# Two load slots for the later modulation's chunks on TensorE, its additions spread anew, and the rotary angles ahead of x

## The reference

```python
for l in range(DEPTH):                                  # DEPTH = 2
    mod = c_act @ w_ada[l] + b_ada[l]                   # c_act = silu(c), one row of 2048; w_ada 2048 x 6144
    shift, scale, gate = jnp.split(mod, 3, axis=-1)
    h = _layernorm(x) * (1.0 + scale[:, None, :]) + shift[:, None, :]
    p = h @ w_in[l]
    u_f, z_f, cq, ckv, k_r, z_a = jnp.split(p, split_pts, axis=-1)
    y_f = _fourier_mix(u_f, w_fmix[l]) * jax.nn.silu(z_f)
    ...                                                 # 8 heads of latent attention, rotary angles from positions
    y = jnp.concatenate([y_f, y_a], axis=-1) @ w_out[l]
    x = _layernorm(DEEPNORM_ALPHA * x + gate[:, None, :] * y, ln_g[l], ln_b[l])
```

## Time and profile before

| | |
|---|---|
| median of 3 runs | 2257.72 us (2253.89 to 2260.4) |
| the profiled execution | 2257.66 us, its span 2255.9 us |
| mean granted clock of TensorE | 0.956 |
| TensorE busy | 2078.6 us (92%) |
| VectorE, ScalarE busy | 1391.3 us (62%), 921.5 us (41%) |
| transfers | 462.27 MB, mean 205 GB/s |

### The profile page before, as it was taken

One profiled execution on the slowest core, in us unless ns is written; L12 is line 12 of the kernel. 1 busy time (PEld: TensorE's weight loads), 2 busy tenths in 40 slices (PEclk: granted clock), 3 DMA queues, 4 the chain that ended last, 5 costly groups with the idle time before them and its releaser, 6 DMA issues.

```text
span 2255.9 us, 37129 instructions
## 1 busy us (share of the span) xinstructions
PE 2078.6 (92%) x14348; PEld 1879.9 (83%) x14348; DVE 1391.3 (62%) x1913; ACT 921.5 (41%) x1355; POOL 26.2 (1%) x53
## 2 busy tenths in 40 slices
PE   6997986887799999879999899999999999999998
PEld 2786875755799997779998899879989989988986
DVE  5365564656657886678899655555545545545555
ACT  2353343412354454344334333445434434434443
POOL 0000000000000000000000000000000000000000
PEclk8998998988899999989999999999999999999999
DMA  9966665676356764525454455553555555555553
GB/s 392 397 262 230 232 249 205 233 280 250 136 201 231 259 230 180 185 96 185 171 184 150 153 182 185 187 205 132 187 202 184 183 193 186 186 192 192 183 196 130
DMA packets 64205, 462.27 MB, mean 205 GB/s; under 512 B 7120, under 2 KB 7632, under 8 KB 8176
## 3 DMA queue, kind: packets, MB, share of 16 engines
q1 hardware_dynamic: 57152, 410.49, 49.5%
q0 software_dynamic: 6960, 50.46, 6.1%
HBM read 458.83 MB, written 2.10 MB: 204 GB/s over the span
## 4 chain that ended last, share of the span: by engine, by line
PE 77%; DVE 12%; DMA 7%; ACT 2%; issue 1%; SPq 0%; ACTq 0%; DVEq 0%; POOLq 0%
PE ps L452 25%; PE ps L453 24%; PE ps L454 24%; DMA area<-in_ada 6%; DVE w_lo L1509 4%; DVE area L1536 2%; PE ps L655 1%; PE ps L608 1%; ACT w_hi L1038 1%; DVE st L1517 1%; DVE X L1940 0%; PE ps L502 0%; DMA raw<-in_stream 0%; DVE X L1934 0%; ACT sc L1269 0%
## 5 line engine op out<-in xcount | busy, mean ns | idle before, releaser
L1509 DVE TENSOR_TENSOR w_lo<-raw,w_hi 128x1024 fp32r<-128x1024 f32 x658 | 777.2, 1221 | 453.3 <-ACT w_hi L1038 451.7
L1038 ACT CAST w_hi<-raw 128x1024 fp32r (+1 forms) x658 | 656.5, 1046 | 558.1 <-PE ps L454 553.4
L452 PE MATMUL ps<-a_hi,w_lo 128*128 128x256 f32 (+1 forms) x2912 | 830.4, 285 | 10.6 <-DVE w_lo L1509 6.7
L453 PE MATMUL ps<-a_lo,w_hi 128*128 128x256 f32 (+1 forms) x2912 | 826.3, 284 | 0.0
L454 PE MATMUL ps<-a_hi,w_hi 128*128 128x256 f32 (+1 forms) x2912 | 824.9, 283 | 0.0
L452 PEld LDWEIGHTS ps<-a_hi,w_lo 128*128 128x128 f32 x2912 | 555.1, 191 | 32.2 <-issue 21.9
L454 PEld LDWEIGHTS ps<-a_hi,w_hi 128*128 128x128 f32 x2912 | 554.6, 190 | 0.0
L453 PEld LDWEIGHTS ps<-a_lo,w_hi 128*128 128x128 f32 x2912 | 552.0, 190 | 0.8 <-issue 0.5
L452 PE MATMUL ps<-w_hi,y_lo 128*128 128x512 f32 x768 | 306.0, 398 | 8.0 <-DVEq L1555 5.4
L453 PE MATMUL ps<-w_lo,y_hi 128*128 128x512 f32 x768 | 303.2, 395 | 0.0
L454 PE MATMUL ps<-w_hi,y_hi 128*128 128x512 f32 x768 | 302.6, 394 | 0.0
(11 more groups left out here) (248 smaller groups left out, 1983.1 us busy)
## 6 DMA issues: line engine op xcount, KB each, us to landing
raw<-in_stream SPq DMA_DIRECT2D x331, 1024.0 KB, 4.8
area<-in_ada SPq DMA_DIRECT2D x56, 1024.0 KB, 7.2
area<-in_ada POOLq DMA_DIRECT2D x40, 1024.0 KB, 5.1
grow<-in_rows POOLq DMA_DIRECT2D x4, 1024.0 KB, 5.6
area<-in_rows POOLq DMA_DIRECT2D x4, 1024.0 KB, 5.2
X<-in_x SPq DMA_DIRECT2D x1, 2048.0 KB, 7.8
out<-X SPq DMA_DIRECT2D x4, 512.0 KB, 2.6
con<-in_consts SPq DMA_DIRECT2D x1, 129.5 KB, 7.7
```

What stands on the lines that cost most here:

```text
L452: pe.matmul(o, w[1], a[0], start=first, stop=False, skip_group_check=shared)
L453: pe.matmul(o, w[0], a[1], start=False, stop=False, skip_group_check=shared)
L1038: ac.copy(to, raw[:, bass.ds((g % RAW) * CH + h * n, n)]).then_inc(hi_ready, 1)
L1509: ve.tensor_tensor(to, raw[:, bass.ds((g % RAW) * CH + h * n, n)], hi.bitcast(F32), ALU.subtract).then_inc(lo_ready, 1)
```

## The change

Five things change.

- TensorE's chunks of the later modulation have two slots: even ones in `area`, odd ones below 20 in `grow`; from 20 on all go to `area`. The load for addition i waits for addition i-2 (i-1 from 21 on) and stands in SyncE's order right behind the weight load four chunks after it. The gate's broadcast row is loaded into `grow` only after TensorE's addition 19. GpSimd's loop over its loads is written out.
- The additions are placed anew. TensorE: 8, 12 and 4 in Fourier groups, heads and output projection, in place of 6, 10 and 8. VectorE: 5, 11 and 8, in place of 5, 7 and 12; three of the heads (0, 3, 5) have two, the second behind the head's last split and ahead of the maximum of the scores.
- The sums that close a row, the copies and the turning of rows move with them (to heads 1 and 7 and chunk 5 of the output projection).
- ScalarE's loop over the heads is written out in both layers.
- In the prologue, the constants, the positions and the meta tokens are loaded ahead of x; VectorE forms the squares' sums and the rotary angles, and ScalarE the sines, before they wait for x. The pieces of the projection start one chunk earlier, the first weight chunks are loaded one chunk earlier, and turning a row stands ahead of the chunk of the next one.

```diff
@@ module level
-PE_ADDS = tuple(L_FOUR + i for i in (7, 8, 10, 11, 12, 14)) \
-    + tuple(L_HEAD + i for i in (1, 3, 5, 7, 8, 9, 11, 12, 13, 15)) \
-    + tuple(L_OUT + i for i in (2, 4, 5, 7, 8, 10, 11, 12))
+PE_ADDS = tuple(L_FOUR + i for i in (7, 9, 10, 11, 12, 13, 14, 15)) \
+    + tuple(L_HEAD + i for i in (1, 3, 4, 5, 7, 8, 9, 11, 12, 13, 14, 15)) \
+    + tuple(L_OUT + i for i in (3, 6, 9, 12))
+PE_BEFORE = {i: i - 2 for i in range(2, 21)} | {i: i - 1 for i in range(21, 24)}
+DVE_HEADS = ((10, 12), (14,), (16,), (18, 20), (22,), (24, 26), (28,), (30,))
+W_ADDS = (0, 2, 3, 5, 6, 8, 9, 11)
@@ build
+        def pe_slot(i):
+            return grow[:, :] if i % 2 and i < 20 else area[:, CH:2 * CH]
@@ SyncE
             sp.dma_start(vec[:, :], vectors).then_inc(vec_in, 16)
+            sp.dma_start(con[:, :], consts).then_inc(con_in, 16)
+            sp.dma_start(pos, positions).then_inc(small, 16)
+            sp.dma_start(mt, meta).then_inc(small, 16)
             sp.dma_start(X[:, :].rearrange("p (t d) -> p t d", t=2), x.rearrange("(t p) d -> p t d", p=P))\
                 .then_inc(x_in, 16)
-            sp.dma_start(con[:, :], consts).then_inc(con_in, 16)
             for c in range(3):
                 sp.dma_start(ada0_slot(c), ada0[c]).then_inc(ada0_landed[c], 16)
-            sp.dma_start(pos, positions).then_inc(small, 16)
-            sp.dma_start(mt, meta).then_inc(small, 16)
...
-            early = {9: 0, 11: 1, 14: 2, 17: 3, 19: 4, 22: 5, 25: 6, 27: 7, 30: 8}
+            early = {8: 0, 10: 1, 13: 2, 16: 3, 18: 4, 21: 5, 24: 6, 26: 7, 29: 8}
...
-                sp.dma_start(ada_ring[:, CH:2 * CH], ada[2 * i + 1]).then_inc(ada_rowed, 16)
+                sp.dma_start(pe_slot(i), ada[2 * i + 1]).then_inc(ada_rowed[i % 2], 16)
...
-                if g - 5 in PE_ADDS[:-1]:
-                    i = PE_ADDS.index(g - 5) + 1
-                    sp.wait_ge(ada_pe, i)
-                    row_weights(i)
+                if g == L_FOUR + 10:
+                    sp.wait_ge(y_mul, 2)
+                    row_weights(1)
+                for i, before in PE_BEFORE.items():
+                    if PE_ADDS[before] == g - 4:
+                        sp.wait_ge(ada_pe, before + 1)
+                        row_weights(i)
@@ GpSimd
-            pool.wait_ge(y_mul, 2)
-            row(grow[:, :], R_GATE, grow_in)
-            with pool.Fori(1, 3 * KT // 2) as i:
+            for i in range(1, 3 * KT // 2):
                 pool.wait_ge(ada_step, i)
                 weights(2 * i, 0)
+                if i == KT:
+                    pool.wait_ge(ada_pe, 20)
+                    row(grow[:, :], R_GATE, grow_in)
@@ TensorE
             def ada_add(n):
...
-                pe.wait_ge(ada_rowed, 16 * (n // 2 + 1))
+                if n == 2 * KT + 1:
+                    pe.wait_ge(row_in, 9)
+                i = n // 2
+                pe.wait_ge(ada_rowed[i % 2], 16 * (i // 2 + 1))
...
+            pe.wait_ge(m_sq, 1)
+            pe.matmul(bank(1, 0, META), ones[:, :], rs[:, 0:META], start=True, stop=True).then_inc(m_acc, 1)
             p = 0
             for c in range(ADA0):
-                ada_chunk(c)
                 if c % 4 == 0 and c:
                     turn_row(c // 4 - 1)
+                ada_chunk(c)
                 if 2 <= c < 6:
                     turn_tokens(0, c - 2)
-                if c == 6:
-                    pe.wait_ge(m_sq, 1)
-                    pe.matmul(bank(1, 0, META), ones[:, :], zs[:, 0:META], start=True, stop=True)\
-                        .then_inc(m_acc, 1)
-                if c == 10:
+                if c == 9:
                     pe.wait_ge(ln_var, NORM["meta"] + 1)
                     pe.wait_ge(xn_l, 4)
-                while p < (c - 10) * 3 // 2:
+                while p < (c - 9) * 3 // 2:
...
-                        if h == 3:
+                        if h == 1:
                             finish_rows(2)
+                        if h == HEADS - 1:
+                            finish_rows(3)
...
-                    if l == 0 and c == 4:
-                        finish_rows(3)
-                    if l == 0 and c == 6:
+                    if l == 0 and c == 5:
                         turn_rows(4, 10)
@@ ScalarE
+                    if l == 0 and h == 2:
+                        take_rows(2)
...
-                head(0, True)
-                with ac.Fori(1, HEADS) as h:
-                    head(h, False)
+                for h in range(HEADS):
+                    head(h, h == 0)
...
-                if l == 0:
-                    take_rows(2)
...
-                    if l == 0 and c == 5:
+                    if l == 0 and c == 3:
                         ac.wait_ge(ada_summed, 1)
                         take_rows(3)
@@ VectorE
-                    elif h < 3:
-                        add_ada(10 + 2 * h, 0, 5 + h)
-                    elif h > 3:
-                        add_ada(8 + 2 * h, 0, 4 + h, 3 if h == 4 else 0)
+                    else:
+                        n = DVE_HEADS[h][0]
+                        add_ada(n, 0, n // 2, 3 if n == KT else 0)
...
+                    if l == 0:
+                        for n in DVE_HEADS[h][1:]:
+                            add_ada(n, 0, n // 2)
...
-                    if l == 0 and c == 8:
+                    if l == 0 and c == 7:
                         read_mod(3, 4, 2)
-                    if l == 0 and (c < 4 or 5 <= c < 13):
-                        n = 24 + 2 * c - 2 * (c > 4)
-                        add_ada(n, 0, n // 2, 4 if c == 5 else 0)
+                    if l == 0 and c in W_ADDS:
+                        n = 2 * KT + 2 * W_ADDS.index(c)
+                        add_ada(n, 0, n // 2, 4 if n == 2 * KT else 0)
```

More of the change, by code:

```diff
@@ L1090, in take_turned @@
                 ac.copy(xn(y_hi, q), bank(turn_banks(0, q)[0], 0, 4 * T)).then_inc(xn_h, 1)
+            ac.wait_ge(rope_arg, 1)
+            ac.activation(rope[:, :], zs[:, :], ACT.Sin).then_inc(rope_sin, 1)
             root("pre0", 0, 1e-6, 2)
@@ L1244, in turned, with take_rows @@
                     ac.copy(pt_hi, bank(3, 0, 2 * T)).then_inc(pt_h, 1)
+                def take_rows(r):
+                    ac.wait_ge(ada_rows, r - 1)
+                    ac.copy(row[:, :], bank(ROW_BANK[r], 0, BLK)).then_inc(row_in, 1)
                 def head(h, first):
@@ L1652, in _ @@
             take_turned(3)
-            ve.wait_ge(small, SMALL)
-            own.link(ve.tensor_tensor(sc[:, 2 * T:2 * T + KT * META], mt, mt, ALU.mult))
-            ve.tensor_reduce(zs[:, 0:META], sc[:, 2 * T:2 * T + KT * META].rearrange("p (k t) -> p t k", k=KT),
-                             AX.X, ALU.add).then_inc(m_sq, 1)
             ve.wait_ge(m_acc, 1)
```

54 lines of the change are left out of this document (27 added, 27 removed).

## The result

The changed kernel takes 2188.13 us in the median (2187.51 to 2189.74, 4 runs) against 2258.92 before: 0.9692 of the time, interval 0.9675 to 0.9708, 70.8 us less. The forecast was 2178, the range 2166 to 2203. In the profiled execution (2188.61 us, span 2186.7) the mean granted clock is 0.973 in place of 0.956.

What follows compares the result with a forecast made beforehand. TensorE's waits (62.4 us) and the half clock after them (25.3) bound three first-layer stages, 87.7 us in all. Gains of 18.3 + 27.9 + 32.5 + 1 = 79.7 took 2257.7 to 2178 us, range 2166 to 2203.

Steps and rivals of the forecast that it cites:

- Two slots: TensorE's row loads in the three stages: a second slot removes the ten waits, 53.5 us in all.
- The one buffer is the reason: TensorE's additions: the next row load can only be issued once the addition before is done, hence the waits.
- Fourier groups: First layer's Fourier groups: 14.7 us of waits and 4.6 of half clock won, less 1: gain 18.3 us.
- Heads: First layer's heads: 23.6 us of waits and 9.3 of half clock won, less 5: gain 27.9 us.
- the landing behind a double head: Heads: VectorE waits 0.7 to 2.7 us for the load behind double heads, with 1.9 us of slack.
- The softmax chain behind the second addition: Heads: the second addition delays TensorE's transposition, up to 1.9 us in head 1, 0.9 each in heads 4 and 6.
- Output projection: First layer's output projection: 35.5 us of waits and half clock won, less 3: gain 32.5 us.
- Prologue: Start of the kernel: small loads and early work give a gain of 1 us, bounds 2 lost and 3 gained.
- VectorE as the bound: Rival, heads and output projection: VectorE becomes the bound, only 56 us won, time about 2202; chance 0.12.
- GpSimd's loads were late: Rival, heads and output projection: landings 2.4 us longer cost 14 and some 5 us more, 2197 us; chance 0.06.
- The clock that the forecast named as its sign: Fourier groups, heads and output projection: granted clock rises from 0.92, 0.90 and 0.88 to 0.98 or more.
- the 0.95 that it had named as a sign of being wrong: The three stages: wrong if the waits go but stages don't get shorter, as when the clock stays below 0.95.

Runs made afterwards that it cites:

- Runs 2 to 6: Before with row loads one chunk earlier, 2208.17; changed with one slot, 2201.67; old places, two slots, 2194.61; that, late loads, 2213.11; changed, late loads, 2198.80 us.
- run 1: The kernel before with only the change's prologue (loads, table and order): 2260.06 us against 2259.70.
- run 8: The changed kernel without 22 of TensorE's 24 row loads, all additions kept: 2172.00 us.
- kernel 10: The changed kernel with VectorE's additions spread evenly over Fourier groups and heads, and respaced in the output projection: 2172.38 us.

## Why the prediction came out as it did

A residue is what the forecast took off a stage's gain for new waits; measured, it is what the removed waits and half clock could have given less what the stage won.

**Two slots.** The ten waits went, as forecast. The reason given, "The one buffer is the reason", is half of it. The prediction named the other half in the same sentence (SyncE comes to the load only behind a weight load that waits for a split) and then gave the whole gain to the slots. Runs 2 to 6 show that the place in the list alone gives 53 us, the slots alone 47, and both 65. A sum over the waits could not tell the two apart; the idle time between the free slot and the issue (5.2 us from 178.00 on; in the earlier trace rows 8.4 us, since that slot was free at 208.70) could have. That the number came out all the same is luck in part: the change also moves the loads up the list, so the sum over the waits was right for both together.

**Fourier groups.** A gain of 18.3 was forecast, with additions moved between stages left out. Measured 17.0, and 19.0 with the two more of TensorE's additions taken off (2.1): the residue was 0.3, not 1.

**Heads.** This term was mis-sized: 27.9 forecast, 10.1 measured, 13.2 if two additions and a closing sum (1.04 each) that moved here are left out. The residue is 19.7 us against 5 taken and a bound of 12. The first three rows of waits above make 12.4 (the fourth, 0.6, stood there before too), and 13.4 us of TensorE's work at half clock another 6.7. The mechanism was the one named, the landing behind a double head. Two figures of its price were wrong. The landing was taken as 5.1, "up to 7 beside others", and was 8.93, 9.45 and 8.69: the median of a queue's loads is not the landing of the one that decides, and the earlier trace rows held one of 8.93. And the slack was read at the half chunk (301.98 against 303.87), while the first consumer behind that addition is `attend`: the low part of the probabilities, behind the same addition and a split. In head 3 of the changed kernel, where nothing waits, that part ends at 304.52 and `attend` starts at 305.11, 0.6 us of slack. The half clock that such waits bring was in the sum for the waits removed, and not in the residues. Nor was the closing sum that the change puts into head 1, behind such an addition: it waits 1.9 us. The softmax chain behind the second addition, which the forecast feared, costs 0.55 us each in heads 4 and 6.

**Output projection.** 32.5 forecast; measured 39.5, and 34.3 with the four additions and the closing sum that left taken off. By the forecast's 35.5 the residue was 1.2, not 3: VectorE waited 5.57 and 3.45 us for landings, and TensorE for none of it. But the earlier trace rows leave out one stretch at half clock of this stage, behind the first run of `turn_rows`. Of the kernel before, from the timeline and the busy times:

```profile
476.01 3.93 PE L626 MATMUL ps<-con,rs 128*128 128x1 f32 x32
479.18:482.60 3.42, 3.42 (x12) 2.84 (x12) 2.69 (x2) 0.00 (x0) 0.00 (x0) 0.50 0.49 163
```

It cost 1.7 us, so 37.2 could be won and the residue was 2.9. The changed kernel has such a stretch too, which costs 3.4 (last section). The gate row behind addition 19 cost nothing.

**Prologue.** A gain of 1 was forecast, with bounds of 2 lost and 3 gained; run 1 shows none, within some 4 us either way.

**Sum.** 79.7 forecast, 70.8 measured: heads 14.7 short, the rest some 6 over. The heads' residue lies outside its own bounds of 2 to 12; the median stays in the range because the bounds of the other terms were wider than what they came to. Of the rivals, VectorE as the bound comes nearest in its place (the heads) but not in its mechanism: run 8, with all of VectorE's work, takes 128.6 us there. GpSimd's loads were late at three places, though run 8 puts that on the overlap with SyncE's loads, not on VectorE, whose work was unchanged in it. The clock that the forecast named as its sign (0.98 or more) came in the groups (1.00), and not in the heads (0.94) nor, at 0.97, in the output projection; the heads' 0.94 is below the 0.95 that it had named as a sign of being wrong.

## What to carry to other kernels

When an engine waits for a load, split the wait in two: from the moment the buffer is free to the issue, and from the issue to the landing. The first part may be only a matter of what stands ahead in the issuing queue, and moving the load up by one place can do most of what a second buffer does.

A chain of load and use in one slot needs its uses spaced by a landing and a use, 11 to 12 us here where loads overlap (8.7 to 9.5 and 2.35). Look at the closest pair, not at the number per stage, and take the landing from the loads that overlap as this one will. Moving what stands behind the late use only moves the wait.

## What the runs showed of the hardware

Over the three stages of all traces, a 1 MB load landed in 4.6 to 5.1 us when no other was under way (but for one of 6.0), in up to 7.7 when at most one other was, up to 10.4 with two others and up to 11.1 with three. In run 8 none took over 7.1, and only 7 of its loads met two others; in the other kernels the longest took 9.2 to 11.1. In the heads of the changed kernel the rate was up to 432 GB/s in slices and 293 in the mean.

The clock also falls without a wait. `turn_rows` is a run of matmuls with one moving column each:

```profile
420.98 4.67 PE L640 MATMUL ps<-con,rs 128*128 128x1 f32 x32
```

TensorE is busy through them, and the granted clock is 0.50 from 423.33 to 430.15, which costs 3.4 us of its 6.82. It is the only half-clock stretch in the output projection of the changed kernel, and no wait stands ahead of it. The kernel before shows the same at 479.18, behind the 32 matmuls from 476.01 on, and kernel 10 from 407.4 to 410.8, behind 32 from 403.75 on. That these matmuls bring the fall is not tested by a run without them.
